# Swapping the start phases of two buffer families: activations at multiples of 128 bytes, split weights 32 bytes past them

## The reference

```
def first_block(x, c, ctx, ...):
    sh1, sc1, gt1, sh2, sc2, gt2 = split(silu(c) @ w_mod + b_mod, 6)
    h, hc = rmsnorm(x, g_attn) * (1 + sc1) + sh1, rmsnorm(ctx, g_attn) * (1 + csc1) + csh1
    cq, ckv, kr, qn, kn, vn, f = split(h @ w_in)          # and the same of hc
    ...                                                   # latent, neighbourhood and Fourier mixing
    x = x + gt1 * (concat([o_mla, o_na, o_fn]) @ w_out)
    h2 = rmsnorm(x, g_ffn) * (1 + sc2) + sh2
    u = conv3(h2 @ w_up)                                  # 2048 x 11264
    gate, val = split(u, 2)
    x = x + gt2 * ((silu(gate) * val) @ w_down)           # 5632 x 2048
    return rmsnorm(x, g_final)

def second_block(x, ...):
    qa, ka, va, qb, kb, vb, ga, gb = split(rmsnorm(x) @ w_in_2)
    merged = sigmoid(ga) * (attn_a @ w_branch_a) + sigmoid(gb) * (attn_b @ w_branch_b)
    x = x + merged @ w_out_2
    x = x + swiglu(rmsnorm(x), w_ffn_in_2, w_ffn_down_2)  # 2048 x 11264 and 5632 x 2048
    return rmsnorm(x)
```

## Time and profile before

| | |
|---|---|
| time before, median of 3 runs | 2622.3 us (2622.0 to 2623.08) |
| profiled execution, own time | 2623.12 us |
| its span | 2621.3 us |
| TensorE matmuls busy | 2581.6 us (98%), 15178 records |
| weight loads busy | 2228.9 us (85%) |
| VectorE busy | 1786.2 us (68%) |
| ScalarE busy | 1218.4 us (46%) |
| read from HBM | 542.68 MB, 208 GB/s over the span |

### The profile page before, as it was taken

How to read it: one execution, slowest core, us unless ns; L and a number is a source line. 1 busy time by engine, 2 the same in 40 slices (tenths; PEclk the granted TensorE clock), 3 DMA queues, 4 the chain that set the end, 5 groups by cost and what they waited for, 6 DMA issues and landing times.

```text
span 2621.3 us, 37078 instructions
## 1 busy us (share of the span) xinstructions
PE 2581.6 (98%) x15178; PEld 2228.9 (85%) x15178; DVE 1786.2 (68%) x2474; ACT 1218.4 (46%) x1605; POOL 32.4 (1%) x31
## 2 busy tenths in 40 slices
PE   6999999999999999999999999999999999999998
PEld 4788778888888888888898888899888888888887
DVE  4367977788888877555656677676766666665555
ACT  4442345455555555444433555545544444444443
POOL 2100000000000000000000000000000000000000
PEclk9999999999999999999999999999999999999999
DMA  9877974767777665565555544465555555555553
GB/s 391 347 301 268 329 236 163 235 211 240 235 239 235 212 194 186 186 196 189 187 187 191 169 138 138 159 193 191 187 186 192 192 188 190 191 188 193 188 190 121
DMA packets 151401, 547.21 MB, mean 209 GB/s; under 512 B 16960, under 2 KB 18880, under 8 KB 150464
## 3 DMA queue, kind: packets, MB, share of 16 engines
q1 hardware_dynamic: 148752, 540.35, 61.3%
q10 hardware_dynamic: 2480, 4.49, 0.6%
HBM read 542.68 MB, written 2.10 MB: 208 GB/s over the span
## 4 chain that ended last, share of the span: by engine, by line
PE 96%; DMA 2%; DVE 1%; issue 0%; ACT 0%; SPq 0%; ACTq 0%; DVEq 0%
PE ps L467 47%; PE ps L466 24%; PE ps L471 3%; PE ps L472 3%; PE ps L473 3%; PE ps L464 3%; PE ps L479 2%; PE ps L477 2%; PE ps L478 2%; DMA raw<-in_stream 2%; PE ps L465 1%; PE ps L1704 1%; PE ps L1913 1%; PE ps L1883 1%; PE ps L1885 1%; PE ps L1900 0%
## 5 line engine op out<-in xcount | busy, mean ns | idle before, releaser
L419 DVE TENSOR_TENSOR lo<-raw,hi 128x1024 fp32r<-128x1024 f32 x814 | 991.3, 1223 | 709.9 <-ACT hi L406 707.8
L467 PE MATMUL ps<-pair,hi 128*128 128x512 f32 x3994 | 1391.4, 392 | 0.0
L406 ACT ACTIVATE hi<-raw 128x1024 fp32r<-128x1024 f32 x814 | 859.5, 1059 | 1069.5 <-PE ps L467 897.0
L466 PE MATMUL ps<-pair,lo 128*128 128x256 f32 x3994 | 1119.8, 280 | 0.0
L467 PEld LDWEIGHTS ps<-pair,hi 128*128 128x128 f32 x3994 | 750.3, 188 | 161.4
L466 PEld LDWEIGHTS ps<-pair,lo 128*128 128x128 f32 x3994 | 750.5, 188 | 6.0 <-issue 2.4
L467 PE MATMUL ps<-hid,hi 128*128 128x512 f32 x1376 | 477.4, 392 | 0.0
L466 PE MATMUL ps<-hid,lo 128*128 128x256 f32 x1376 | 384.6, 280 | 0.0
L467 PEld LDWEIGHTS ps<-hid,hi 128*128 128x128 f32 x1376 | 258.3, 188 | 56.7
L466 PEld LDWEIGHTS ps<-hid,lo 128*128 128x128 f32 x1376 | 258.3, 188 | 0.3
L1299 DVE TENSOR_REDUCE tmp<-ps 128x256 f32<-128x512 f32 x260 | 176.4, 683 | 5.0 <-PE ps L467 4.6
(11 more groups left out here) (328 smaller groups left out, 2299.4 us busy)
## 6 DMA issues: line engine op xcount, KB each, us to landing
raw<-in_stream SPq DMA_DIRECT2D x983, 512.0 KB, 4.2
raw_deep<-in_stream SPq DMA_DIRECT2D x31, 512.0 KB, 11.0
xc<-in_xc SPq DMA_DIRECT2D x4, 1024.0 KB, 8.1
x<-in_x ACTq DMA_DIRECT2D x1, 2048.0 KB, 7.6
out<-out_sb SPq DMA_DIRECT2D x8, 256.0 KB, 3.0
c_bc<-in_c_bc SPq DMA_DIRECT2D x1, 1024.0 KB, 11.7
bias<-in_rpb ACTq DMA_DIRECT2D x4, 256.0 KB, 4.6
dft<-in_dft_tab ACTq DMA_DIRECT2D x1, 512.0 KB, 5.8
```

Source lines behind the costliest of these rows:

```text
L406: e.activation(hi[:, c % R, :], raw_of(p), ACT.Copy).then_inc(hi_ready, 1)
L419: e.tensor_tensor(lo[:, c % R, :], raw_of(p), hi[:, c % R, :].bitcast(F32), ALU.subtract)\
L466: e.matmul(out[:, T:2 * T], wlo, act[:, 0, :], start=False, stop=False)
L467: return e.matmul(out, whi, both_, start=False, stop=last)
```

## The change

One line is added ahead of `hi`, and one line ahead of `pair` has another target.

```
--- before
+++ after
@@ -223,6 +223,7 @@

         K1 = 1024
         raw, _ = place("raw", [P, RR, CH])
+        top[0] += (32 - top[0]) % 128
         hi, _ = place("hi", [P, R, CH], F32R)
         lo, _ = place("lo", [P, R, CH], F32R)
         x, home = place("x", [P, KT, T])
@@ -245,7 +246,7 @@
         small, _ = place("small", [P, 8 * 24])
         rope, rope_at = place("rope", [P, 2 * T + P])
         cos, sin, rot = rope[:, 0:T], rope[:, T:2 * T], rope[:, 2 * T:2 * T + P]
-        top[0] += (32 - top[0]) % 128
+        top[0] += -top[0] % 128

         pair, both_at = place("pair", [P, KT, 2, T], F32R)
         reg = top[0]
```

## The result

The changed kernel takes 2641.63 us (median of 4 runs, 2641.28 to 2642.08) against 2622.64 us: 1.0071 times as long, with an interval of 1.0059 to 1.0083. That is 19.0 us slower, inside the stated range and well outside the likeliest case's own range.

What follows compares the result with a forecast made beforehand. TensorE's matmul spacing was taken to bound 95% of the time. 5632 x (-1.0 + 1.2) ns = +1.1 us on the 2622.3 us median gave 2623.4 us, other terms about nothing; range 2611 to 2645 us.

Steps and rivals of the forecast that it cites:

- the stated range: Whole kernel: 2611 to 2645 us, from the doubled gain to the price of the weight load, leaving two in ten out.
- the likeliest case: TensorE in `features`: two terms of opposite sign, 2623.4 us, own range 2614 to 2632 us; chance 0.40.
- What bounds the kernel: For 95% of the time, the distance from one TensorE matmul's start to the next one's counts.
- VectorE and ScalarE at nothing: Chunk work on these engines: phase costs nothing, and any cost is hidden; mean chunk times stay within 1%.
- DMA at nothing: Transfers to `raw` and `raw_deep` in the DMA-bound start: phase costs 0, with 1 us either way allowed.
- The swap read off `three` against `tokens`: TensorE: swapped phases make 512-column matmuls 1.0 ns shorter and 256-column ones 1.2 ns longer.
- The step that failed: In `features`: 5632 pairs times (-1.0 + 1.2) ns, giving +1.1 us.
- the slow rival: Weight loads at phase 32 touch five blocks, not four: 2.0 ns on each of 11,264 matmuls, 2645 us; chance 0.29.
- No dependence on phase: Whole kernel: phases that are multiples of 16 change nothing, 2622.3 us; chance 0.08.
- the moving read gains: In `features`, streamed reads at phase 0 gain and weight loads don't pay: -5.6 to -11.3 us, 2611 to 2617; chance 0.23.
- What was named as the way to be wrong: TensorE matmuls: the price depends on the two phases together, for which `tokens` is no image; no size given.
- The other way to be wrong that was named: Ring buffers: the price depends on the match between reader and writer of one buffer; no size given.

Runs made afterwards that it cites:

- experiment 1: Against the kernel before the change, only the activations moved, from phase 32 to 0, with the rings staying at 0; 2645.3 us, ratio 1.0086.
- experiment 3: Against the kernel before the change, activations moved to phase 96, rings staying at 0; 2644.4 us, ratio 1.0083.
- experiment 9: Against the kernel before the change, rings moved to phase 32 and activations to 64; 2622.76 us against 2622.52, ratio 1.0001.
- experiment 10: Against the kernel before the change, hi and lo begin 512 bytes further up, phases unchanged; 2622.85 us, ratio 0.9999.
- experiment 12: Against the kernel before the change, hi and lo start at phase 112 in buffers 128 bytes longer, activations at 32; 2610.49 us, ratio 0.9953.
- experiment 11: Against the kernel before the change, hi and lo start at phase 16 in buffers 128 bytes longer, activations at 32; 2654.59 us, ratio 1.0118.

## Why the prediction was right in its range and wrong in its likeliest case

**What bounds the kernel: right.** The change acted through the spacing of matmuls and through nothing else of that size: the start alone moved too, by -1.3 us. TensorE's two longest waits are 18.1 and 6.1 us, where they were 17.9 and 6.1.

**VectorE and ScalarE at nothing: right. DMA at nothing: slightly off.** Chunks take 1224 ns on VectorE against 1223. The start, up to the `ckvn` product, came 1.3 us shorter, and only 1 us either way was allowed for. Whether the phase of `raw_deep` does this is not shown: in experiment 1, where it is at 0 too, the last matmul over it begins 0.6 us earlier than before, and over the other experiments this start ranges from 120.58 to 121.19 us, one trace each.

**The swap read off `three` against `tokens`: right for these helpers.** 512 columns: forecast 1.0 ns shorter in `three`, measured 0.9 (234.3 to 233.4), and the reverse in `tokens`, measured +1.1. 256 columns in `three`: forecast +1.2 with ends at -0.4 and +2.7, measured +1.2 over `cqn` and +2.6 over `pair`.

**The step that failed** is the one that multiplied these by 5632: "`three` against `tokens`, at equal width, is the nearest pair of rows for the price of the swap", carried over to `features`. There the 512-column matmul got 3.0 ns longer where -1.0 was forecast, and the 256-column one 0.4 longer where 1.2 was. The sum was -1.0 + 1.2 = +0.2 ns a pair, measured +3.4. Rows of before already showed that `features` is no mixture of the other two: a pair takes 346.7 ns, while `three` at both widths adds up to 234.3 + 118.0 = 352.3 ns. The kernel before had a spacing in `features` that no row of `three` or `tokens` priced. I used the difference of two rows for a group whose absolute value neither row matched.

**That the time lies in the range is luck.** The upper end was the price of the slow rival. **That rival, "the weight load pays for phase 32", had the right sign and nearly the right size** (2645 against 2641.6 us) **and the wrong mechanism.** With rings at 0 the kernel is as slow (experiments 1 and 3), with rings at 32 as quick as before (experiment 9). *No dependence on phase* fell with the result, and *the moving read gains* too: 512 columns at phase 0 take more.

**What was named as the way to be wrong is what happened**: the price depends on the two phases together. The two sixes of `tokens` led me to suspect address bits of 128 and above; experiment 10 shows that 512 bytes do not count for `features`, and 128 and 256 stay open. The other way to be wrong that was named, reader against writer of one buffer, can be checked in the traces at hand. I sorted the 512-column matmuls over `hid` by what ran from 200 ns before their start to 100 ns after the next one's. With ScalarE idle and VectorE busy the spacing is 229.10 ns before and 232.21 after; with VectorE idle and ScalarE busy it is 229.19 and 232.19 (250 to 357 matmuls each). With both idle, 12 matmuls each, it is 229.2 and 232.5. So the 3 ns do not come from the writing of the rings.

**Shown:** in this kernel, with both rings at one phase, the spacing in `features` follows the distance from the rings to the activations and not the phase of either, and 512 bytes more or less don't change it: three kernels at distance 0 agree within 0.02 ns a matmul, two at 96 (the changed one is one of them), four at 32. By phase distance a pair takes 351.1 (0), 353.3 (16), 346.7 (32), 344.5 (48), 353.3 (64) and 350.1 ns (96).

**Open:** why, and with what period. That a stream and a load that run side by side get in each other's way would fit a dependence on the distance alone, but no run separates the two, and no rule that I can give predicts the six values, or 231.86 and 234.03 ns where the rings differ. No two kernels differ in distance by 128 or 256 bytes alone, so that the price repeats every 128 bytes is an assumption. Phase distances 80 and 112 were not tried, nor others that are no multiple of 16, nor the rings at 48 with another offset between `hi` and `lo`. In experiment 12 `lo` also stands 128 bytes further from `hi`, and the activations 256 bytes further up; experiment 11 has the same and is slow, so this is not what makes it quick, but its share was not measured apart.

## What to carry to other kernels

When matmuls follow one another without a wait, each with its own weight load, the start addresses of the streamed and the loaded buffer are a tuning knob worth up to 1.7% here from the worst to the best placement (2654.6 to 2610.5 us), and 0.5% against the kernel before, with no instruction changed. Sweep the distance between the two families in steps of 16 bytes, over 512 bytes, since nothing here shows a shorter period, and in the real sequence of matmuls: moving one family is enough, and another helper ranks the distances differently. Before a price is carried from one group of matmuls to another, check that the rows also give the absolute spacing of the group it is carried to.

## What the runs showed of the hardware that was not expected

- Two placements of the same program, differing only in addresses, differ by 44 us of 2622 (distance 48 against 16).
- Moving only one family costs more (2645.3 and 2647.0 us) than moving both in opposite directions (2641.6).
- A phase distance that is no multiple of 32 gives both the best and one of the two worst spacings, 344.5 and 353.3 ns.
- The order of the distances differs from helper to helper. `features` is slowest at distances 16 and 64, and there `tokens` over `ckvn` is quickest: by the time stamps 227.6 and 227.9 ns after a `hi` matmul, against 234.3 at distance 32. `tokens` also swaps the roles, but `three` has those of `features`, and over `cqn` a `hi` matmul of 256 columns takes 113.2 ns at distance 64 against 118.5 at 32. Whether the mix of widths or the order of the slices does this was not separated.
